# A one-core decoder step: the last down projection takes tokens 256 to 519 first, and the final norm is scaled on three engines and stored partly as half rows

## The chip, the cores and the metric

The kernel runs on one core of one Trainium2 chip. The metric is the time of the program on the device in microseconds (us), shown as the median of several runs. A profiled execution has a time of its own and a span, which runs from its first to its last instruction; all rows below are from that execution, in microseconds from the start of its span.

## The reference, cut to what matters

One decoder layer is computed for 512 prompt tokens and 8 sample tokens (520 in all) of width 1024: a norm, an input projection, block-sparse attention and mLSTM side by side, an output projection, and a squared-ReLU MLP. A last RMS norm over each token's 1024 values gives the two main outputs:

```python
hn = rmsnorm(x, ln2_w)
x = x + jnp.square(jax.nn.relu(hn @ w_up)) @ w_down
...
y_prompt = rmsnorm(xp, lnf_w)      # (1, 512, 1024)
y_sample = rmsnorm(xs, lnf_w)      # (8, 1, 1024)
```

where `rmsnorm` multiplies a token's row by the reciprocal square root of its mean square (plus 1e-6) and by the weights. The change touches nothing but the end of the MLP's down projection and this last norm.

## The kernel before, in words

Each engine has a program of its own, in the order in which it is written; semaphores join them. TensorE (PE) multiplies, VectorE (DVE) and ScalarE (ACT) move results out of PSUM and do the elementwise work, GpSimd (POOL) splits weights and raises to powers, SyncE (SP) issues nearly all loads and the final stores.

The activations lie transposed in `xT`: 128 partitions, 8 feature tiles, 520 tokens. The last phase of the MLP (`down_last`) runs over the 8 feature tiles `t`. Each tile has two token halves of 260, `H0` and `H1`, and each half is 24 matmuls: 8 steps `k`, each as three products of high and low parts (`down_part`). When a half is done, DVE adds it to `xT` (`evac_add`), ACT squares it into `y_sq` (`y_square`), and DVE adds the squares of tiles 0 to 6 up in `y_sum` (`add_squares`).

The final norm works by token tiles, numbered 0 to 3 (128 prompt tokens each) and 4, called `NT` (the 8 samples):

- `y_to_tok(i, part)`: PE transposes four feature tiles of token tile `i` into one PSUM bank. Part 0 (features 0 to 511) is done inside `down_last`, and DVE writes it, times the norm weights `lnf_b`, to the left half of `y_out` (`y_first`). Part 1 (features 512 to 1023) needs the last feature tile.
- `y_sums(part)`: PE multiplies `y_sum` and `y_sq` by a column of ones, which gives each token's sum of squares. Part 0 holds tiles 0 and 1 and stands inside the last half, after step 5; part 1 holds tiles 2, 3 and `NT` and waits for the square of the last half.
- `y_mean(part)`: DVE scales the sums to mean squares in `y_ms`; POOL raises them to the power -0.5 (`rsqrt`, counted by `s_y_pow`).
- DVE then multiplies the right half of a row by `y_ms` and `lnf_b` while it moves it out of PSUM, ACT multiplies the left half by `y_ms` (`y_scale`, counted by `s_y_half`), and SP stores whole rows of 4 KB, one DMA for each token tile, in the order 0, 1, 2, 3, `NT`.

PSUM banks of the final norm are handed out in the order of a list of jobs (`plan`); a job in the same bank waits until the job four places earlier has been read (`free`, `evacuated`).

Of the kernel before, what the change touches and what calls it, by code (L numbers as in the profile page):

```python
# [31 lines left out]
P = 128  # L32
# [43 lines left out]
Y_TILES = (0, 1), (2, 3, NT)  # L76
# [72 lines left out]
def plan():  # L149
# [107 lines left out]
    for part in range(2):  # L257
        job("ysum", part)
        for i in Y_TILES[part]:
            job("yt", i, 1)  # L260
# [132 lines left out]
def build(nc, x_prompt, x_sample, cache_k, cache_v, page_table, state_C, state_n, state_m, ln1_w, w_in,  # L393
# [4 lines left out]
    with ctx:  # L398
# [276 lines left out]
        s_y_half = sem("y_half")  # L675
        s_y_stored = sem("y_stored")
# [118 lines left out]
        def _(sp):  # L795
# [115 lines left out]
        def _(pe):  # L911
# [429 lines left out]
            def y_sums(part):  # L1341

                pe.wait_ge(s_y_added, KT - 2)
                pe.wait_ge(s_y_sq, KT + part)
                out = open_job(pe, "ysum", part)
                for i in Y_TILES[part]:
                    n = P if i < NT else NS
                    cols = slice(i * P, i * P + n)
                    pe.matmul(out[0:n, i:i + 1], y_sum[:, cols], ones[:, :], start=True, stop=False)
                    mm = pe.matmul(out[0:n, i:i + 1], y_sq[:, 1, cols], ones[:, :], start=False, stop=True)  # L1350
                done(mm)
# [60 lines left out]
            def down_part(b, half, n, k, first, last, signal):  # L1412

                out, cols = mlp_bank(b)[:, 0:MH_TOK], (H0, H1)[half]
# [7 lines left out]
            def down(d, i=0):  # L1422

                pe.wait_ge(s_hs_lo, 4 * (d + 1) + 8 * i)
                for t in range(8):
                    n = FIRST["down", d] + t
                    lo_made(pe, n, i)
                    for half in range(2):
                        bank_free("down", d, 2 * t + half, i)
                        for k in range(4):  # L1430
                            down_part(BANKS["down", d, 2 * t + half][0], half, n, 4 * (d % 2) + k, k == 0, k == 3,
                                      None if k < 3 else s_u_done if half else s_dn0)

            def down_last():

                for t in range(8):
# [8 lines left out]
                    for half, k in steps:  # L1445
# [4 lines left out]
                        down_part(2 * (t % 2) + half, half, n + k // 4, k, k == 0, k == KT - 1,  # L1450
                                  s_u_done if half and k in (3, 7) else s_dn0 if k == KT - 1 else None)
                        if t == 7 and half == 1 and k == 5:
                            y_sums(0)
# [53 lines left out]
        def _(act):  # L1507
# [349 lines left out]
            def down(kind, d, i=0):  # L1857

                for t in range(8):
# [6 lines left out]
                    elif kind == "last":  # L1866
                        for half in range(2):
                            y_square(t, (H0, H1)[half], 16 * 6 + 2 * t + half + 1)
# [9 lines left out]
            def y_scale(i):  # L1878

                n = P if i < NT else NS  # L1880
                evacuated(act, "yt", i, 0)
                act.wait_ge(s_y_pow, 1 if i in Y_TILES[0] else 3 if i == NT else 2)
                act.activation(y_out[0:n, i, 0:512], y_out[0:n, i, 0:512], ACT.Copy, scale=y_ms[0:n, i:i + 1])\
                   .then_inc(s_y_half, 1)
# [20 lines left out]
            for i in range(NT + 1):  # L1905
                y_scale(i)
# [12 lines left out]
        def _(pool):  # L1919
# [143 lines left out]
            for what, e in PHASES[11:]:  # L2063
                phase(what, e)
            evacuated(pool, "ysum", 0)
            rsqrt(y_ms[:, 0:2], P, 2).then_inc(s_y_pow, 1)
# [6 lines left out]
        def _(dve):  # L2073
# [445 lines left out]
            def evac_add(kind, d, t, half):  # L2519

                x = xT[:, t, (H0, H1)[half]]
                dve.tensor_tensor(x, mlp_bank(BANKS[kind, d, 2 * t + half][0])[:, 0:MH_TOK], x, ALU.add)\  # L2522
# [219 lines left out]
            def y_mean(part):  # L2742
                out = full(dve, "ysum", part)
                if part == 0:
                    free(dve.tensor_scalar(y_ms[:, 0:2], out[:, 0:2], 1.0 / D, EPS, ALU.mult, ALU.add), "ysum", 0)
                else:
                    dve.tensor_scalar(y_ms[:, 2:NT], out[:, 2:NT], 1.0 / D, EPS, ALU.mult, ALU.add)\
                       .then_inc(s_y_ms_ok, 1)
                    dve.tensor_scalar(y_ms[0:NS, NT:NT + 1], out[0:NS, NT:NT + 1], 1.0 / D, EPS, ALU.mult, ALU.add)\
                       .then_inc(s_y_ms_ok, 1)  # L2750
# [15 lines left out]
            for part in range(2):  # L2766
                if part == 1:
                    y_mean(1)
                for i in Y_TILES[part]:
                    n = P if i < NT else NS  # L2770
                    out = full(dve, "yt", i, 1)
                    dve.wait_ge(s_y_pow, 1 if part == 0 else 3 if i == NT else 2)
                    free(dve.scalar_tensor_tensor(out=y_out[0:n, i, 512:D], in0=out[0:n, :],
                                                  scalar=y_ms[0:n, i:i + 1], in1=lnf_b[0:n, 512:D],
                                                  op0=ALU.mult, op1=ALU.mult), "yt", i, 1)
# [26 lines left out]
```

## Time and profile before

| | before |
|---|---|
| time, median of 3 runs | 699.6 us (699.0 to 699.85) |
| time of the profiled execution | 699.11 us |
| its span | 697.4 us |
| PE, DVE, ACT, POOL busy | 681.3, 449.9, 296.3, 322.6 us |
| granted TensorE clock | 1.000 |

The profiled execution takes 1.7 us longer than its span. The busy times are sums over the whole span; the change lies in its last 15 us, so the rows that matter are those of that stretch.

### The profile page before, as it was taken

The page shows a single profiled execution, that of the slowest core. Times are in us where ns is not written, and L with a number is a line of the kernel's source. Part 1 is how long each engine was busy: PE and PEld are TensorE (multiplying, and loading weights), DVE is VectorE, ACT ScalarE, POOL GpSimd, SP SyncE. Part 2 cuts the span into 40 slices and gives each one's busy share as a digit, 9 for nine tenths or more (in the row PEclk, how much of TensorE's full clock was granted, in tenths as well). Part 3 has the DMA queues.
Part 4 walks back from the last instruction along what each step waited for, and adds up shares of the span by engine and source line. Part 5 has one row for each costly group of instructions (what it writes and reads, how often), then busy time and mean ns, then how long its engine had stood idle before and what let it go on. Part 6 is the DMA issues. An engine that isn't in the chain of part 4 may idle for free.

```text
span 697.4 us, 15167 instructions
## 1 busy us (share of the span) xinstructions
PE 681.3 (98%) x5547; PEld 638.8 (92%) x5547; DVE 449.9 (65%) x894; ACT 296.3 (42%) x568; POOL 322.6 (46%) x232
## 2 busy tenths in 40 slices
PE   6999999999999999999999999999999999999996
PEld 6999988788687777999999999999999999999996
DVE  4598899986243456537798685867557576585134
ACT  6532735465342233245555443343433534334222
POOL 6739999823231544247337517062260623507431
PEclk9999999999999999999999999999999999999999
DMA  7946999944486788623111323332241331413103
GB/s 246 303 122 168 281 282 277 277 136 116 143 254 204 239 283 172 168 81 122 61 59 64 121 70 127 109 118 86 87 124 69 120 108 66 130 61 121 61 1 124
DMA packets 88633, 100.41 MB, mean 144 GB/s; under 512 B 5374, under 2 KB 64338, under 8 KB 88570
## 3 DMA queue, kind: packets, MB, share of 16 engines
q1 hardware_dynamic: 74566, 92.91, 42.9%
q10 hardware_dynamic: 14004, 6.67, 4.1%
q8 instruction: 39, 0.64, 0.4%
q14 instruction: 24, 0.20, 0.1%
HBM read 92.92 MB, written 6.64 MB: 143 GB/s over the span
## 4 chain that ended last, share of the span: by engine, by line
PE 80%; DVE 10%; issue 3%; POOL 3%; ACT 2%; DMA 1%; DVEq 0%; POOLq 0%; ACTq 0%
PE acc L914 7%; PE acc L915 6%; PE acc L916 6%; PE acc L1417 5%; PE acc L1418 5%; PE acc L1416 5%; PE scr L1417 3%; PE scr L1418 3%; PE scr L1416 3%; PE scr L1383 3%; PE scr L1382 3%; PE scr L1384 3%; PE acc L1382 3%; PE acc L1383 3%; PE acc L1384 3%
## 5 line engine op out<-in xcount | busy, mean ns | idle before, releaser
L914 PE MATMUL acc<-act_hi,w_hi 128*128 128x256 f32 (+1 forms) x416 | 120.8, 290 | 1.1 <-DVE zT L2503 1.1
L2017 POOL TENSOR_TENSOR h_lo<-relu,h_hi 128x520 fp32r<-128x520 f32 x32 | 44.0, 1379 | 164.8 <-ACT h_hi L1803 164.5
L915 PE MATMUL acc<-act_lo,w_hi 128*128 128x256 f32 (+1 forms) x416 | 117.3, 282 | 0.0
L916 PE MATMUL acc<-act_hi,w_lo 128*128 128x256 f32 (+1 forms) x416 | 117.2, 282 | 0.0
L1502 POOL TENSOR_TENSOR w_lo<-raw,w_hi 128x1024 fp32r<-128x1024 f32 x24 | 57.2, 2387 | 97.6 <-ACT w_hi L1495 95.2
L1970 POOL TENSOR_TENSOR prod<-kv,Qb 128x1024 f32<-128x1024 f32 x32 | 85.7, 2714 | 14.1 <-DVE S L2205 11.1
L914 PEld LDWEIGHTS acc<-act_hi,w_hi 128*128 128x128 f32 x416 | 78.4, 188 | 4.0 <-issue 2.3
L915 PEld LDWEIGHTS acc<-act_lo,w_hi 128*128 128x128 f32 x416 | 78.4, 189 | 0.5
L916 PEld LDWEIGHTS acc<-act_hi,w_lo 128*128 128x128 f32 x416 | 78.3, 188 | 0.0
L2522 DVE TENSOR_TENSOR xT<-acc,xT 128x260 f32<-128x260 f32 x64 | 26.7, 426 | 48.4 <-PE acc L1418 48.4
L2503 DVE TENSOR_TENSOR zT<-acc,rstd 128x264 f32<-128x264 f32 (+1 forms) x56 | 23.5, 421 | 43.1 <-PE acc L916 40.4
L1416 PE MATMUL acc<-h_hi,w_hi 128*128 128x260 f32 x176 | 49.9, 283 | 0.0
L1495 ACT ACTIVATE w_hi<-raw 128x1024 fp32r<-128x1024 f32 x36 | 37.8, 1056 | 28.2 <-PE acc L916 14.0
L1417 PE MATMUL acc<-h_lo,w_hi 128*128 128x260 f32 x176 | 49.7, 282 | 0.0
L1418 PE MATMUL acc<-h_hi,w_lo 128*128 128x260 f32 x176 | 49.7, 282 | 0.0
L1791 ACT ACTIVATE w_hi<-w_sum 128x512 fp32r<-128x512 f32 x35 | 21.4, 628 | 65.0 <-DVE w_sum L2537 50.2
L2024 POOL TENSOR_TENSOR w_lo<-raw,w_hi 128x512 fp32r<-128x512 f32 x21 | 31.0, 1491 | 37.8 <-ACT w_hi L1791 37.8
L1802 ACT ACTIVATE relu<-relu 128x520 f32<-128x520 f32 x32 | 20.3, 636 | 64.8 <-DVE relu L2610 64.7
L2205 DVE TENSOR_REDUCE S<-prod 128x16 f32<-128x1024 f32 x32 | 38.4, 1210 | 8.2 <-POOL prod L1970 8.1
L1417 PE MATMUL acc<-h_lo,u_hi 128*128 128x260 f32 x144 | 40.7, 283 | 0.0
L1417 PE MATMUL scr<-h_lo,w_hi 128*128 128x260 f32 x144 | 40.7, 283 | 0.0
L1416 PE MATMUL acc<-h_hi,u_hi 128*128 128x260 f32 x144 | 40.7, 282 | 0.0
(418 smaller groups left out, 2298.4 us busy)
## 6 DMA issues: line engine op xcount, KB each, us to landing
kv<-in_cache_k_dram SPq DMA_DIRECT2D x64, 256.0 KB, 3.4
kv<-in_cache_v_dram SPq DMA_DIRECT2D x64, 256.0 KB, 3.1
raw<-in_w_up_dram SPq DMA_DIRECT2D x16, 1024.0 KB, 5.5
raw_d<-in_w_down_dram SPq DMA_DIRECT2D x12, 1024.0 KB, 5.1
raw<-in_w_in_dram SPq DMA_DIRECT2D x14, 512.0 KB, 6.0
raw<-in_w_in_dram SPq DMA_DIRECT2D x7, 1024.0 KB, 7.4
x_tok<-in_x_prompt_dram SPq DMA_DIRECT2D x8, 512.0 KB, 5.3
raw<-in_w_out_dram SPq DMA_DIRECT2D x4, 1024.0 KB, 7.3
```

Source lines behind the costliest of these rows:

```text
L914: pe.matmul(out, W_HI[home(g)][:, k, :], hi[k][:, cols], start=(n == 0), stop=False)
L915: pe.matmul(out, W_HI[home(g)][:, k, :], lo[k][:, cols], start=False, stop=False)
L916: mm = pe.matmul(out, W_LO[home(g)][:, k, :], hi[k][:, cols], start=False, stop=(n == KT - 1))
L1382: pe.matmul(out, u_hi[n % RING][:, k, :], hi[k], start=(k == 0), stop=False)
L1383: pe.matmul(out, u_hi[n % RING][:, k, :], lo[k], start=False, stop=False)
L1384: mm = pe.matmul(out, u_lo[n % RING][:, k, :], hi[k], start=False, stop=(k == 3))
L1416: pe.matmul(out, w[0], h_hi[:, k, cols], start=first, stop=False)
L1417: pe.matmul(out, w[0], h_lo[:, k, cols], start=False, stop=False)
L1418: mm = pe.matmul(out, w[1], h_hi[:, k, cols], start=False, stop=last)
L1502: eng.tensor_tensor(W_LO[home(g)], raw[:, r_slot, :, side * P:(side + 1) * P], W_HI[home(g)].bitcast(F32), ALU.subtract).then_inc(s_w_lo_o ...
L1970: pool.tensor_tensor(prod[:, n % 2, :].rearrange("p (j n) -> p j n", j=2), kv[:, 2 * c:2 * c + 2, :], Qb[:, b % 2:b % 2 + 1, :].to_broadca ...
L2017: pool.tensor_tensor(h_lo[:, t, :], relu2[:, t % 2, :], h_hi[:, t, :].bitcast(F32), ALU.subtract).then_inc(s_hs_lo, 1)
```

## The change

In the last phase, the two halves of a tile become tokens 256 to 519 (264 of them, first) and tokens 0 to 255 (256, last). The first sums of squares are those of tiles 2, 3 and `NT`, after step 3 of the last half. The sums of tiles 0 and 1 are made in two jobs, `ypre` (tiles 0 to 6, which doesn't wait for the last square) and `ysum` 1 (the last feature tile alone), and DVE joins them. The left half of tile 2 and all of the samples' last factors go to POOL; ACT takes the left halves of tiles 3, 0 and 1 and moves the samples' right half out of PSUM. Tiles 2 and 3 are stored as whole rows by SP, tiles 0 and 1 as two half rows each: the left one by ACT's queue, the right one by SP's. SP's order is 2, 3, 0, `NT`, 1.

```diff
-Y_TILES = (0, 1), (2, 3, NT)
+Y_SPLIT = slice(2 * P, TOK), slice(0, 2 * P)
+Y_TILES = (2, 3, NT), (0, 1)
...
-            for i in range(NT + 1):
-                sp.wait_ge(s_y_half, i + 1)
+            for i in (2, 3, 0, NT, 1):
+                if i == NT:
+                    sp.wait_ge(s_y_pool, 3)
+                    sp.dma_start(y_sample[:, 0, :], y_out[0:NS, i, :]).then_inc(s_y_stored, 16)
+                    continue
                 evacuated(sp, "yt", i, 1)
-                if i < NT:
+                if i >= 2:
+                    if i == 2:
+                        sp.wait_ge(s_y_pool, 1)
+                    else:
+                        sp.wait_ge(s_y_half, 1)
                     sp.dma_start(y_prompt[0, i * P:(i + 1) * P, :], y_out[:, i, :]).then_inc(s_y_stored, 16)
                 else:
-                    sp.dma_start(y_sample[:, 0, :], y_out[0:NS, i, :]).then_inc(s_y_stored, 16)
-            sp.wait_ge(s_y_stored, 16 * (NT + 1))
+                    sp.dma_start(y_prompt[0, i * P:(i + 1) * P, 512:D], y_out[:, i, 512:D]).then_inc(s_y_stored, 16)
+            sp.wait_ge(s_y_stored, 16 * (NT + 3))
...
                 pe.wait_ge(s_y_added, KT - 2)
+                if part == 1:
+                    out = open_job(pe, "ypre")
+                    for i in Y_TILES[1]:
+                        mm = pe.matmul(out[:, i:i + 1], y_sum[:, i * P:(i + 1) * P], ones[:, :], start=True, stop=True)
+                    done(mm)
+                    for i in (2, 3):
+                        y_to_tok(i, 1)
                 pe.wait_ge(s_y_sq, KT + part)
...
-                        if t == 7 and half == 1 and k == 5:
+                        if t == 7 and half == 1 and k == 3:
                             y_sums(0)
...
             pe.wait_ge(s_dn_evac, N_DOWN - 1)
-            for i in Y_TILES[0]:
-                y_to_tok(i, 1)
             y_sums(1)
+            y_to_tok(NT, 1)
             pe.wait_ge(s_dn_evac, N_DOWN)
             for i in Y_TILES[1]:
                 y_to_tok(i, 1)
...
+            def y_scale(i, pows, nth):
+
                 evacuated(act, "yt", i, 0)
-                act.wait_ge(s_y_pow, 1 if i in Y_TILES[0] else 3 if i == NT else 2)
...
+                act.wait_ge(s_y_pow, pows)
+                x = y_out[:, i, 0:512]
+                act.activation(x, x, ACT.Copy, scale=y_ms[:, i:i + 1]).then_inc(s_y_half, 1)
+                if i < 2:
+                    act.wait_ge(s_y_half, nth)
+                    act.dma_start(y_prompt[0, i * P:(i + 1) * P, 0:512], x).then_inc(s_y_stored, 16)
...
-            for i in range(NT + 1):
-                y_scale(i)
+            y_scale(3, 1, 1)
+            act.wait_ge(s_y_pow, 2)
+            y_samples()
+            y_scale(0, 3, 2)
+            y_scale(1, 3, 3)
...
+            pool.wait_ge(s_y_ms_ok, 1)
+            rsqrt(y_ms[:, 2:NT], P, 2).then_inc(s_y_pow, 1)
             evacuated(pool, "ysum", 0)
+            rsqrt(y_ms[0:NS, NT:NT + 1], NS, 1).then_inc(s_y_pow, 1)
...
+                x = y_out[0:n, i, 0:512]
+                pool.tensor_tensor(x, x, y_ms[0:n, i:i + 1].to_broadcast([n, 512]), ALU.mult).then_inc(s_y_pool, 1)
+
+            y_scale(2, P, 1)
+            pool.wait_ge(s_y_ms_ok, 2)
             rsqrt(y_ms[:, 0:2], P, 2).then_inc(s_y_pow, 1)
-            pool.wait_ge(s_y_ms_ok, 2)
-            rsqrt(y_ms[:, 2:NT], P, 2).then_inc(s_y_pow, 1)
-            rsqrt(y_ms[0:NS, NT:NT + 1], NS, 1).then_inc(s_y_pow, 1)
+            y_scale(NT, NS, 2)
+            pool.wait_ge(s_y_nt, 1)
+            x = y_out[0:NS, NT, 512:D]
+            pool.tensor_tensor(x, x, lnf_b[0:NS, 512:D], ALU.mult).then_inc(s_y_pool, 1)
...
+                    dve.scalar_tensor_tensor(out=y_ms[:, 0:2], in0=out[:, 0:2], scalar=1.0 / D, in1=y_ms[:, 0:2],
+                                             op0=ALU.mult, op1=ALU.add).then_inc(s_y_ms_ok, 1)
```

PE from the last matmul ahead of the first sums of squares to its end, before (`ones` with `y_sum` or `y_sq` are the sums of squares, `ident` with `xT` the transposes; line numbers are each kernel's own):

```order
L1418 MATMUL acc<-h_hi,w_lo 128x260
L1349 MATMUL scr<-ones,y_sum 128x1 [waits scr_free0,y_sq,y_added]
L1350 MATMUL scr<-ones,y_sq 128x1
...
L1338 MATMUL scr<-ident,xT 128x128 [waits scr_free1,dn_evac]
L1338 MATMUL scr<-ident,xT 128x128 [waits scr_free2]
L1349 MATMUL scr<-ones,y_sum 128x1 [waits scr_free3,y_sq,y_added]
L1349 MATMUL scr<-ones,y_sum 8x1
L1338 MATMUL scr<-ident,xT 128x128 [waits scr_free0,dn_evac]
L1338 MATMUL scr<-ident,xT 8x128 [waits scr_free2]
```

The same stretch of PE in the changed kernel:

```order
L1439 MATMUL acc<-h_hi,w_lo 128x256
L1370 MATMUL scr<-ones,y_sum 128x1 [waits scr_free0,y_sq,y_added]
L1371 MATMUL scr<-ones,y_sq 128x1
L1370 MATMUL scr<-ones,y_sum 8x1
...
L1360 MATMUL scr<-ones,y_sum 128x1 [waits scr_free1,y_added,dn_evac]
L1351 MATMUL scr<-ident,xT 128x128 [waits scr_free2]
L1351 MATMUL scr<-ident,xT 128x128 [waits scr_free3]
L1371 MATMUL scr<-ones,y_sq 128x1 [waits scr_free0,y_sq]
L1351 MATMUL scr<-ident,xT 8x128 [waits scr_free1]
L1351 MATMUL scr<-ident,xT 128x128 [waits scr_free2,dn_evac]
```

Six matmuls of the last half moved behind the first sums, which now hold the samples too; the `ypre` job went in between the last half and the first transposes.

POOL's last rows, before and in the changed kernel:

```order
L2024 TENSOR_TENSOR w_lo<-raw,w_hi 128x512 [waits u_hi] x7
L2024 TENSOR_TENSOR u_lo_109<-raw,u_hi_106 128x512 [waits u_hi]
L2024 TENSOR_TENSOR w_lo<-raw,w_hi 128x512 [waits u_hi] x2
L1922 TENSOR_TENSOR y_ms<-y_ms,power 128x2 [waits scr_free0]
L1922 TENSOR_TENSOR y_ms<-y_ms,power 128x2 [waits y_ms_ok]
L1922 TENSOR_TENSOR y_ms<-y_ms,power 8x1
```

```order
L1953 TENSOR_TENSOR y_ms<-y_ms,power 128x2 [waits y_ms_ok]
L1953 TENSOR_TENSOR y_ms<-y_ms,power 8x1 [waits scr_free0]
L2106 TENSOR_TENSOR y_out<-y_out,y_ms 128x512 [waits y_pow,scr_free1]
L1953 TENSOR_TENSOR y_ms<-y_ms,power 128x2 [waits y_ms_ok]
L2106 TENSOR_TENSOR y_out<-y_out,y_ms 8x512 [waits y_pow,scr_free3]
L2114 TENSOR_TENSOR y_out<-y_out,lnf_b 8x512 [waits y_nt]
```

Three multiplications of 512 columns joined the three powers; the samples' two stand last.

SP's final stores, before and in the changed kernel:

```order
L904 DMA out_dram<-y_out 128x1024 [waits scr_free1,y_half]
L904 DMA out_dram<-y_out 128x1024 [waits scr_free2,y_half]
L904 DMA out_dram<-y_out 128x1024 [waits scr_free0,y_half]
L904 DMA out_dram<-y_out 128x1024 [waits scr_free1,y_half]
L906 DMA out_dram<-y_out 8x1024 [waits scr_free2,y_half]
```

```order
L917 DMA out_dram<-y_out 128x1024 [waits y_pool,scr_free2]
L917 DMA out_dram<-y_out 128x1024 [waits y_half,scr_free3]
L919 DMA out_dram<-y_out 128x512 [waits scr_free2]
L909 DMA out_dram<-y_out 8x1024 [waits y_pool]
L919 DMA out_dram<-y_out 128x512 [waits scr_free3]
```

The samples' store moved ahead of the last prompt tile's, and the last two prompt stores are half as wide; their other halves are two new stores of 128x512 in ACT's program.

## Rows read from the trace of the kernel before

**Rows 1.** The page's head: span, and busy us of each engine.

```profile
span 697.4 us, 15167 instructions
...
PE 681.3 (98%) x5547; PEld 638.8 (92%) x5547; DVE 449.9 (65%) x894; ACT 296.3 (42%) x568; POOL 322.6 (46%) x232
```

**Rows 2.** The chain of waits, last 12 us: start, us, what.

```profile
692.67 0.65 DVE y_out L2773
```

**Rows 3.** Timeline of DVE, ACT, POOL, SP: start, us, engine, line, operation; waits in brackets.

```profile
687.95 0.43 DVE L2522 TENSOR_TENSOR xT<-acc,xT 128x260 f32<-128x260 f32 x1 [0.67 <-PE acc L1418]
688.39 1.41 DVE L2773 SCALAR_TENSOR_TENSOR y_out<-scr,y_ms,lnf_b 128x512 f32<-128x512 f32 x2
...
691.26 2.06 DVE L2773 SCALAR_TENSOR_TENSOR y_out<-scr,y_ms,lnf_b 128x512 f32<-128x512 f32 x3 [0.88 <-POOL y_ms L1922]
...
685.26 0.42 ACT L1775 ACTIVATE y_sq<-xT 128x260 f32<-128x260 f32 x1 [3.30 <-DVE xT L2522]
688.41 0.42 ACT L1775 ACTIVATE y_sq<-xT 128x260 f32<-128x260 f32 x1 [2.73 <-DVE xT L2522]
688.74 1.32 ACT L1883 ACTIVATE y_out<-y_out,y_ms 128x512 f32<-128x512 f32 x2
...
687.36 0.70 POOL L1922 TENSOR_TENSOR y_ms<-y_ms,power 128x2 f32<-128x2 f32 x1 [15.01 <-DVE y_ms L2745]
690.46 1.20 POOL L1922 TENSOR_TENSOR y_ms<-y_ms,power 128x2 f32<-128x2 f32 x2 [2.40 <-DVE y_ms L2749]
...
689.47 3.61 SPq L904 DMA_DIRECT2D out_dram<-y_out  x4
693.39 0.43 SPq L906 DMA_DIRECT2D out_dram<-y_out  x1
```

**Rows 4.** Windows of the end: busy time by engine, PEclk, DMA share, GB/s.

```profile
690.30:691.60 1.30, 1.29 (x12) 0.93 (x10) 0.42 (x3) 0.35 (x1) 1.14 (x2) 1.00 0.99 400
694.20:695.50 1.30, 0.00 (x0) 0.00 (x0) 0.00 (x0) 0.00 (x0) 0.00 (x0) 1.00 1.02 403
696.00:696.60 0.60, 0.00 (x0) 0.00 (x0) 0.00 (x0) 0.00 (x0) 0.00 (x0) 1.00 0.05 14
696.60:697.40 0.80, 0.00 (x0) 0.00 (x0) 0.00 (x0) 0.00 (x0) 0.00 (x0) 0.70 0.00 0
```

**Rows 5.** Timeline of PE, its weight loads (PEld) and one DVE row.

```profile
683.99 0.28 PE L1416 MATMUL acc<-h_hi,w_hi 128*128 128x260 f32 x1
...
686.02 0.31 PEld L1349 LDWEIGHTS scr<-ones,y_sum 128*128 128x128 f32 x2
...
686.91 0.19 PEld L1416 LDWEIGHTS acc<-h_hi,w_hi 128*128 128x128 f32 x1
...
687.64 0.90 PEld L1338 LDWEIGHTS scr<-ident,xT 128*128 128x128 f32 x8
...
688.90 0.30 PEld L1349 LDWEIGHTS scr<-ones,y_sum 128*128 128x128 f32 x2 [0.35 <-issue]
...
690.06 1.24 PEld L1338 LDWEIGHTS scr<-ident,xT 128*128 128x128 f32 x12
...
690.17 0.16 DVE L2747 TENSOR_SCALAR y_ms<-scr 128x2 f32<-128x2 f32 x1 [0.37 <-PE scr L1350]
```

**Rows 6.** Groups of PE instructions by shape: count, busy us, mean ns.

```profile
L915 PE MATMUL acc<-act_lo,w_hi 128*128 128x256 f32 x224 | 62.8, 281 | 0.0
...
L915 PE MATMUL acc<-act_lo,w_hi 128*128 128x264 f32 x192 | 54.5, 284 | 0.0
```

**Rows 7.** Groups of POOL instructions by shape, of the whole span.

```profile
L1970 POOL TENSOR_TENSOR prod<-kv,Qb 128x1024 f32<-128x1024 f32 x32 | 85.7, 2714 | 14.1 <-DVE S L2205 11.1 <-ACT Qb L1562 1.9 <-DMA kv<-in_cache_k_dram 1.0
...
L2024 POOL TENSOR_TENSOR w_lo<-raw_d,w_hi 128x512 fp32r<-128x512 f32 x30 | 38.5, 1308 | 0.0
...
L1995 POOL TENSOR_TENSOR Cs_z<-Cs_z,sm_b 128x512 f32<-128x512 f32 x4 | 4.1, 1048 | 0.0
```

**Rows 8.** A window of loads in rows of 2 KB, columns as in rows 4.

```profile
504.00:506.00 2.00, 2.00 (x19) 2.00 (x19) 0.86 (x2) 0.74 (x2) 2.00 (x3) 1.00 1.04 404
```

More of the change, by code:

```diff
@@ L256, in plan @@
         job("yt", i, 0)
[L257 to L260, printed above, removed]
+    job("ysum", 0)
+    job("ypre")
+    for i in (2, 3):
+        job("yt", i, 1)
+    job("ysum", 1)
+    for i in (NT, 0, 1):
+        job("yt", i, 1)
     return tasks, jobs
@@ L1348, in y_sums @@
                     cols = slice(i * P, i * P + n)
-                    pe.matmul(out[0:n, i:i + 1], y_sum[:, cols], ones[:, :], start=True, stop=False)
-                    mm = pe.matmul(out[0:n, i:i + 1], y_sq[:, 1, cols], ones[:, :], start=False, stop=True)
+                    if part == 0:
+                        pe.matmul(out[0:n, i:i + 1], y_sum[:, cols], ones[:, :], start=True, stop=False)
+                    mm = pe.matmul(out[0:n, i:i + 1], y_sq[:, 1, cols], ones[:, :], start=(part == 1), stop=True)
                 done(mm)
@@ L1410, in plain, with down_part @@
                         norm_to_rows()
-            def down_part(b, half, n, k, first, last, signal):
-                out, cols = mlp_bank(b)[:, 0:MH_TOK], (H0, H1)[half]
+            def down_part(b, cols, n, k, first, last, signal):
+                out = mlp_bank(b)[:, 0:cols.stop - cols.start]
                 w = u_hi[n % RING][:, k % 4, :], u_lo[n % RING][:, k % 4, :]
@@ L2519, in evac_add @@
             def evac_add(kind, d, t, half):
-                x = xT[:, t, (H0, H1)[half]]
-                dve.tensor_tensor(x, mlp_bank(BANKS[kind, d, 2 * t + half][0])[:, 0:MH_TOK], x, ALU.add)\
+                cols = (Y_SPLIT if kind == "last" else (H0, H1))[half]
+                x = xT[:, t, cols]
+                dve.tensor_tensor(x, mlp_bank(BANKS[kind, d, 2 * t + half][0])[:, 0:cols.stop - cols.start], x, ALU.add)\
                    .then_inc(s_dn_evac, 1)
@@ L2743, in y_mean @@
                 out = full(dve, "ysum", part)
[L2744 to L2750, printed above, removed]
+                if part == 1:
+                    evacuated(dve, "ypre")
+                    dve.scalar_tensor_tensor(out=y_ms[:, 0:2], in0=out[:, 0:2], scalar=1.0 / D, in1=y_ms[:, 0:2],
+                                             op0=ALU.mult, op1=ALU.add).then_inc(s_y_ms_ok, 1)
+                    return
+                dve.tensor_scalar(y_ms[:, 2:NT], out[:, 2:NT], 1.0 / D, EPS, ALU.mult, ALU.add).then_inc(s_y_ms_ok, 1)
+                free(dve.tensor_scalar(y_ms[0:NS, NT:NT + 1], out[0:NS, NT:NT + 1], 1.0 / D, EPS, ALU.mult, ALU.add),
+                     "ysum", 0)
             def y_first(i):
@@ L2765, in _ @@
                 phase(what, e)
-            for part in range(2):
-                if part == 1:
+            out = full(dve, "ypre")
+            free(dve.tensor_scalar(y_ms[:, 0:2], out[:, 0:2], 1.0 / D, EPS, ALU.mult, ALU.add), "ypre")
+            for i in (2, 3, 0, 1):
+                if i == 3:
                     y_mean(1)
[L2769 to L2775, printed above, removed]
+                out = full(dve, "yt", i, 1)
+                dve.wait_ge(s_y_pow, 1 if i >= 2 else 3)
+                free(dve.scalar_tensor_tensor(out=y_out[:, i, 512:D], in0=out[:, :], scalar=y_ms[:, i:i + 1],
+                                              in1=lnf_b[:, 512:D], op0=ALU.mult, op1=ALU.mult), "yt", i, 1)
 _INS = ["x_prompt", "x_sample", "cache_k", "cache_v", "page_table", "state_C", "state_n", "state_m", "ln1_w",
```

19 lines of the change are left out of this document (12 added, 7 removed).

## The prediction

> **What bounds the kernel now.** I read the page's head first [rows 1], then the chain of waits [rows 2], the timeline of each engine over the last 15 us [rows 3], the windows of that stretch [rows 4], and PE's timeline [rows 5]. PE is busy for 681.3 of the 697.4 us [rows 1], and the change leaves its work alone up to the last half of the last feature tile; only the tail counts. The chain of waits names DVE's last multiplication, which ends at 693.32 [rows 2]. That is misleading: the span ends 4.1 us later, at 697.4, and the windows say why. From 690.3 to 695.5, in each stretch of 1.3 us of which the first and the last are shown, the 16 DMA engines are busy for 0.99 to 1.02 of the time and move 400 GB/s [rows 4]. One token tile is 0.524 MB, so 1.31 us, and four tiles are 5.2 us, which is that whole stretch. SP issues its first store at 689.47 [rows 3], packets run 0.83 us later, and from there on the tail is a queue of stores: compute that finishes earlier inside it gains nothing. Behind the four tiles come the eight sample rows, 32 KB alone on the engines, and they are slow: the last packets run until 696.6 [rows 4], 1.1 us after the bulk. From there to the end of the span are 0.8 us without a packet [rows 4]. So three numbers make the end: when the first store is issued, 2.13 MB at 400 GB/s, and what follows the last bulk packet.
>
> **The change part by part, in the clock of this trace.**
>
> *Widths.* A matmul of 256 columns is 281 ns, one of 264 is 284 [rows 6]; halves of 260 and 260 become 264 and 256, so a tile costs the same. The first half of the last tile ends about 0.04 late, the second catches up.
>
> *First sums after step 3.* The last half starts at 683.99, and 18 matmuls later, at 686.02, PE loads for the first sums [rows 5]: 0.113 us each. After 12 it is there at 683.99 + 0.04 + 1.36 = 685.39. It needs the square of the first half, which ACT ends at 685.26 + 0.42 = 685.68 [rows 3], 0.04 later now; from ACT's other half square (end 688.83) to PE's load (688.90) were 0.07 [rows 3, 5]. So PE waits until 685.79, a new stall of 0.4 us, with the last 12 matmuls queued behind it. Before, that wait was covered by the six matmuls that are now behind. The sums of three tiles took from 688.90 to 690.06, 1.16 us [rows 5], against 0.89 for two (686.02 to 686.91). The matmuls go on at 686.95, as before at 686.91, but there are 12 instead of 6: 0.7 us more. The last half ends 0.7 us late, and PE is free at 687.64 + 0.74 = 688.38; DVE adds the half at 688.68 instead of 687.95.
>
> *`ypre` and the transposes.* Two tiles with one product each are half of 0.89, so 0.45: PE's transposes of tile 2 start at 688.83. Before, from the first transpose load (687.64) to DVE's multiplication out of that bank (688.39) were 0.75 [rows 3, 5], so DVE starts on tile 2 at 689.58 and ends at 690.33, by 0.75 for one (2.06 for three with overlap [rows 3]). SP follows 0.07 later, as after the last tile (693.32 to 693.39 [rows 3]): first store at **690.40**, 0.93 us later than 689.47.
>
> *POOL's share of the first store.* The first sums reach DVE 1.27 after their load (688.90 to 690.17 [rows 5]), at 687.06, and POOL's power can start at 687.3, as before (687.36). Two powers take 1.20 [rows 3], to 688.5. Then the multiplication of tile 2 by a broadcast column: the nearest row is the state decay, 128x512 by a broadcast, 1.05 us; two full operands take 1.31 [rows 7]. It ends between 689.5 and 689.8. It costs nothing, since DVE's multiplication (690.33) covers it; the first store would feel it only if it ran over 0.5 us longer, and then by the excess. ACT's tile 3 (0.71, half of 1.32 with overlap) ends near 690.2, under the same cover.
>
> *Second sums.* The last half's square ends at 688.68 + 0.45 + 0.42 = 689.55; PE is in its transposes until 689.71 (8 in 0.90 [rows 5]), then sums two tiles in 0.45. DVE's joined `y_ms` follows at about 690.4 (0.16), POOL's power at 690.6, done at 691.3 against 691.16 before: 0.15 late. DVE's tiles 0 and 1 end at 692.15 and 692.85, ACT's left halves at 692.25 and, behind its own store issue (0.4, as SP's last one, 0.43 [rows 3]), at 693.4.
>
> *Samples.* POOL multiplies them twice after 691.3. Partition count is no measure of time on DVE (its three rows of 2.06 include the 8-row one [rows 3]); for POOL I take the full-width rows, 1.05 and 1.31 [rows 7]: done at 693.7. SP's sample store is issued at 693.7, takes 0.43 [rows 3], and the right half of tile 1 waits behind it on SP's queue until 694.15.
>
> *Do the stores arrive in time?* Engines: tile 2 from 690.40 + 0.83 = 691.23, then tile 3 until 693.85, tile 0 until 695.16, tile 1's left half until 695.8. Packets of tile 3 are there at 692.1, of tile 0 at 693.1, of tile 1's left half at 694.3, of its right half at 694.98. Each is earlier than its turn, so the stretch has no gap. Rows of 2 KB ran at 404 GB/s at a DMA share of 1.04 [rows 8], so half rows cost nothing; the second queue's issue on ACT saves SP 0.35 us that nobody waits for.
>
> *Sum.* 691.23 + 2.13 MB / 400 GB/s (5.3) = 696.55; the sample rows now lie in the middle. They took 1.1 us at the end; on the way they cost between 0 (the other queue fills in) and 1.1 us (the last half row waits behind them on their engines). I take 0.3, nearer to the lower end, as ACT's half row lies in another queue. Plus 0.8 to the end: 697.65 against 697.4, so **+0.25 us**: the first store costs 0.93, the sample tail gives 1.1 back, and 0.3 and roundings return. On the profiled 699.11 that is 699.4; the median shown is 0.5 above the profiled run, so I say 699.9.
>
> **A rule against the change.** The windows show all 16 engines busy with one queue alone [rows 4], so a second queue has nothing to fill. The Trainium skill, "DMA: Bandwidth & Descriptors", section "Issuing engines are not separate DMA queues", says the same in general: transfers started by several engines run on the same 16 DMA engines, and only the starter's time is saved. By that rule the sum stands; without it the first rival below would be the forecast. No run here shows two queues in this stretch.
>
> **The rivals.**
>
> *A second queue adds bandwidth.* ACT's two half rows, 0.52 MB, move beside SP's stores: 5.3 becomes 4.0, the end 696.35, and the time 698.6 (-1.05). For it: two queues have never been seen in this tail. Against it: a share of 0.99 to 1.02 [rows 4]. Chance 0.08.
>
> *The sample rows stand in the way in full.* The last half row is issued behind them on the same queue; 0.8 us more, 700.7. For it: SP's order, and their 1.1 us for 32 KB [rows 4]. Chance 0.15.
>
> *SP is held by POOL (slower).* SP can't issue tile 1's right half before POOL's two sample multiplications. The engines want it by 691.23 + 4.68 = 695.9, so issued by 695.1 and the pair done by 694.6: it decides once the pair takes over 3.3 us. If each took what 128x1024 takes, 2.71 [rows 7], the pair would end at 696.7, the half row be issued at 697.2, and with 0.83, 0.65 for its packets and 0.8 the end is 699.5: +2.1, 701.7. For it: these are POOL's first 8-row multiplications of this length, and rows there spread. Against it: 1.05 to 1.31 for full width. Chance 0.10.
>
> **How the numbers follow.** My forecast, a queue of stores that starts 0.9 later and ends about where it did, has 0.67. Its own range: the first store up to 0.45 earlier if PE's wait is not there, and 0.3 later if DVE is slowed beside POOL; the sample rows 0 instead of 0.3, or up to 0.8 more; so 699.1 to 701.0, with 0.3 on either side for how runs spread (699.0 to 699.85 before). For 8 times in 10 I give 698.8 to 701.0. 0.2%, 1.4 us, is about what a measurement of this kernel can tell from no change. Faster than 698.2: a little of the first rival, 0.05. Slower than 701.0: most of the third and a little of the second, 0.10. Same: 0.85.
>
> **What would show it.** In the profile after: PE idle for about 0.4 us ahead of the first sums; the last half's evacuation 0.7 late; first store near 690.4; DMA share near 1 from 691.2 without a hole until about 696.5; POOL's sample pair near 2.4 us; the last packets no longer a thin tail of 1.1 us. I would be wrong if the stretch had holes, if the first store came near 689.5, or if the tail after the bulk stayed as long.

## The result, and the profile after

| | before | after |
|---|---|---|
| time, median | 699.0 us (22 runs) | 700.33 us (22 runs, 699.56 to 701.5) |
| profiled execution, its span | 699.11, 697.4 us | 700.07, 698.3 us |
| first store issued | 689.47 | 690.31 |
| first and last packet of the stores | 690.33, 696.65 | 691.17, 697.49 |
| last packet to end of span | 0.74 | 0.86 |

The ratio is 1.0018, with a 95% interval of 1.0012 to 1.0024: within the 0.2% that the prediction called no change, but over 22 runs a small slowdown that is clear of 1. The two profiled executions differ by 0.96 us, the medians by 1.3. (A packet is what one DMA engine moves in one record, here one row of 4 KB or one half row of 2 KB. Here and below, first and last packet are start and end of the first and last record among the DMA packets behind 688.5 us.) Two runs of the kernels below were far slower at a lower granted clock (a3 1113.18 us at 0.56, a4 742.57 us at 0.85), and their medians and ratios leave them out.

The timeline of the changed kernel, last 14 us: start, us, engine, line, operation, waits in brackets.

```profile
685.82 0.30 PEld L1370 LDWEIGHTS scr<-ones,y_sum 128*128 128x128 f32 x2 [0.39 <-issue]
...
688.38 0.53 PEld L1360 LDWEIGHTS scr<-ones,y_sum 128*128 128x128 f32 x4
688.75 0.94 PEld L1351 LDWEIGHTS scr<-ident,xT 128*128 128x128 f32 x8
...
684.25 0.70 DVE L2786 TENSOR_TENSOR y_sum<-y_sum,y_sq 128x520 f32<-128x520 f32 x1 [1.63 <-PE acc L1439]
...
688.70 0.42 DVE L2568 TENSOR_TENSOR xT<-acc,xT 128x256 f32<-128x256 f32 x1 [1.40 <-PE acc L1439]
...
689.53 0.75 DVE L2820 SCALAR_TENSOR_TENSOR y_out<-scr,y_ms,lnf_b 128x512 f32<-128x512 f32 x1 [0.34 <-PE scr L1351]
...
687.32 1.22 POOL L1953 TENSOR_TENSOR y_ms<-y_ms,power 128x2 f32<-128x2 f32 x2 [14.95 <-DVE y_ms L2795]
688.52 1.03 POOL L2106 TENSOR_TENSOR y_out<-y_out,y_ms 128x512 f32<-128x512 f32 x1
...
691.22 1.03 POOL L2106 TENSOR_TENSOR y_out<-y_out,y_ms 8x512 f32<-8x512 f32 x1
692.21 1.26 POOL L2114 TENSOR_TENSOR y_out<-y_out,lnf_b 8x512 f32<-8x512 f32 x1
...
690.31 1.22 SPq L917 DMA_DIRECT2D out_dram<-y_out  x2
...
693.50 0.31 SPq L909 DMA_DIRECT2D out_dram<-y_out  x1
693.85 0.74 SPq L919 DMA_DIRECT2D out_dram<-y_out  x1
```

Read against [rows 3, 5], the front is what was predicted: PE waits 0.39 us ahead of the first sums, the last half is added at 688.70 (predicted 688.68), DVE reaches tile 2 at 689.53 (689.58), the first store goes at 690.31 (690.40). POOL's left half of tile 2 ends at 689.55, under DVE's cover. Its two sample multiplications take 1.03 and 1.26 us, as long as full-width rows; they end at 693.47, SP issues the samples at 693.50 (693.7), and the right half of tile 1 follows at 693.85 (694.15).

The windows of the end of the changed kernel, columns as in [rows 4].

```profile
691.20:692.50 1.30, 0.66 (x4) 0.42 (x4) 1.14 (x2) 0.92 (x2) 1.30 (x3) 1.00 1.00 403
692.50:693.80 1.30, 0.00 (x0) 0.00 (x0) 0.27 (x1) 0.72 (x1) 0.97 (x1) 1.00 1.00 392
693.80:695.10 1.30, 0.00 (x0) 0.00 (x0) 0.00 (x0) 0.00 (x0) 0.00 (x0) 0.84 1.01 377
695.10:696.40 1.30, 0.00 (x0) 0.00 (x0) 0.00 (x0) 0.00 (x0) 0.00 (x0) 0.50 1.01 314
696.40:696.60 0.20, 0.00 (x0) 0.00 (x0) 0.00 (x0) 0.00 (x0) 0.00 (x0) 0.50 1.00 369
696.60:697.00 0.40, 0.00 (x0) 0.00 (x0) 0.00 (x0) 0.00 (x0) 0.00 (x0) 0.50 0.51 195
697.00:697.50 0.50, 0.00 (x0) 0.00 (x0) 0.00 (x0) 0.00 (x0) 0.00 (x0) 0.50 0.17 61
697.50:698.30 0.80, 0.00 (x0) 0.00 (x0) 0.00 (x0) 0.00 (x0) 0.00 (x0) 0.50 0.00 0
```

There is no hole, as predicted. But the stretch is no shorter. From 695.1 the engines are busy at 314 GB/s instead of about 400: some packets take long. Then, where the kernel before has a thin tail [rows 4], there is a thick one that fades: 0.51, then 0.17. From first to last packet are 6.32 us in both kernels. The store queue starts 0.84 us later, takes as long, and that is the loss but for 0.12 us behind the last packet. (Over all profiles here that last gap is 0.73 to 1.16 us, so the 0.12 may be scatter.) The prediction had the stretch 0.8 us shorter (1.1 given back, 0.3 kept). The experiments ask where these 0.8 us stayed.

### The profile page after: what moved, and what is told of

It reads as the page before. It is cut to its first block, busy times and chain, and to the rows that moved or that the text cites. A ratio compares the mean times of both kernels' runs of the same rounds, so it can differ in the third digit from the quotient of the medians.

```text
span 698.3 us, 15169 instructions
## 1 busy us (share of the span) xinstructions
PE 681.8 (98%) x5547; PEld 639.4 (92%) x5547; DVE 449.3 (64%) x894; ACT 295.9 (42%) x567; POOL 326.0 (47%) x235
## 4 chain that ended last, share of the span: by engine, by line
PE 78%; DVE 10%; POOL 4%; issue 3%; ACT 2%; DMA 1%; SPq 0%; POOLq 0%; ACTq 0%; DVEq 0%
PE acc L927 6%; PE acc L928 6%; PE acc L929 6%; PE acc L1438 5%; PE acc L1437 5%; PE acc L1439 5%; POOL prod L2001 4%; PE scr L1438 3%; PE scr L1439 3%; PE scr L1437 3%; PE scr L1404 3%; PE scr L1403 3%; PE scr L1405 3%; PE acc L1403 3%; PE acc L1405 3%
## 5 line engine op out<-in xcount | busy, mean ns | idle before, releaser
L2568 DVE TENSOR_TENSOR xT<-acc,xT 128x260 f32<-128x260 f32 (+1 forms) x64 | 26.7, 427 | 49.2 <-PE acc L1439 49.2
L1437 PE MATMUL acc<-h_hi,w_hi 128*128 128x260 f32 (+2 forms) x176 | 50.0, 284 | 0.0
L1438 PE MATMUL acc<-h_lo,w_hi 128*128 128x260 f32 (+2 forms) x176 | 49.7, 283 | 0.0
L1439 PE MATMUL acc<-h_hi,w_lo 128*128 128x260 f32 (+2 forms) x176 | 49.7, 282 | 0.0
L1437 PE MATMUL acc<-h_hi,u_hi 128*128 128x260 f32 (+2 forms) x144 | 40.7, 283 | 0.0
L1438 PE MATMUL acc<-h_lo,u_hi 128*128 128x260 f32 (+2 forms) x144 | 40.7, 283 | 0.0
```

What stands on the lines that cost most here:

```text
L1437: pe.matmul(out, w[0], h_hi[:, k, cols], start=first, stop=False)
L1438: pe.matmul(out, w[0], h_lo[:, k, cols], start=False, stop=False)
L1439: mm = pe.matmul(out, w[1], h_hi[:, k, cols], start=False, stop=last)
```

## The experiments

The profiled executions differ in how early they come to the tail at all (by up to 1.6 us, from work ahead of the change). So I count from the start of DVE's last adding of squares (684.19 in the kernel before, 684.25 after), called A here:

```profile
684.19 0.70 DVE L2740 TENSOR_TENSOR y_sum<-y_sum,y_sq 128x520 f32<-128x520 f32 x1 [1.60 <-PE acc L1418]
```

"Store" is the first store's issue behind A, "stretch" first to last packet, "slowest" the longest 4-KB packet in it. A ratio is to runs of the kernel before on the same chip and comes from all of them, so it is not quite the quotient of two medians; medians of before were 699.11 us for the first four kernels, 698.87 for the next four, 699.09 for three, 699.03 for the last.

| kernel | median us | ratio (95%) | store | stretch | slowest ns |
|---|---|---|---|---|---|
| before | 699.0 | 1 | 5.28 | 6.32 | 953 |
| after | 700.33 | 1.0018 (1.0012, 1.0024) | 6.06 | 6.32 | 898 |
| a1_no_sample_store | 699.94 | 1.0013 (1.0004, 1.0021) | 6.07 | 5.94 | 200 |
| a2_sample_rows_spread | 700.04 | 1.0013 (1.0004, 1.0022) | 6.07 | 6.12 | 647 |
| a3_sums_after_step_5 | 699.77 | 1.0010 (1.0002, 1.0019) | 5.63 | 6.31 | 933 |
| a4_whole_rows | 700.34 | 1.0018 (1.0010, 1.0027) | 6.07 | 6.21 | 1041 |
| b1_before_no_sample | 698.75 | 0.9997 (0.9988, 1.0006) | 5.28 | 5.80 | 262 |
| b2_whole_rows_no_sample | 699.57 | 1.0010 (1.0001, 1.0019) | 6.06 | 5.81 | 351 |
| b5_half_rows_one_queue | 700.12 | 1.0015 (1.0006, 1.0024) | 6.06 | 5.91 | 335 |
| b3_step_5_transposes_first | 699.88 | 1.0013 (1.0004, 1.0022) | 5.64 | 6.32 | 701 |
| c1_order_alone | 699.48 | 1.0009 (1.0000, 1.0018) | 5.51 | 6.10 | 989 |
| c2_tile_2_on_act | 699.91 | 1.0007 (0.9998, 1.0016) | 5.22 | 6.69 | 816 |
| c3_before_rows_spread | 698.82 | 0.9996 (0.9987, 1.0005) | 5.28 | 5.98 | 355 |
| d1_order_two_sums | 699.06 | 1.0000 (0.9991, 1.0009) | 5.26 | 6.08 | 898 |

An interval is some 0.6 us to either side, so the ratios tell only the larger steps apart; the columns of the profile carry the argument, with one profile for each kernel. I take them to be good to about 0.1 us: three kernels with whole rows and the sample store in the middle gave 6.08, 6.10 and 6.21.

**The theory and the rival at first.** Mine: the sample store in the middle stands in the way, and the changed kernel without it ends like the kernel before. The rival: half rows or the second queue make the stretch longer.

**a1_no_sample_store**: the sample output is left out.

```
-sp.dma_start(y_sample[:, 0, :], y_out[0:NS, i, :]).then_inc(s_y_stored, 16)
```

> The changed kernel without the store of the eight sample rows (y_sample is not written). My theory: the tail is a queue of stores on busy DMA engines, and the samples' slow packets hold up what is queued behind them in full. Then the first store stays near 690.3, the last packet comes near 696.6 instead of 697.5, the span is 697.4 instead of 698.3, and the ratio to the kernel before is about 1.0005. Rival, half rows in two queues are what is slow: last packet near 697.4, span 698.2, ratio 1.0017.

Missed: the stretch fell by 0.38 us, not by 0.8 or more, and its windows still end in a tail. The sample rows are a part of the cause only.

**a2_sample_rows_spread**: the sample output gets eight rows of tile 3, from partitions 16 apart.

```
-sp.dma_start(y_sample[:, 0, :], y_out[0:NS, i, :])
+sp.dma_start(y_sample[:, 0, :], y_out[0:P:16, 3, :])
```

> The changed kernel, but the sample store takes eight rows that lie 16 partitions apart (rows of token tile 3, so y_sample's values are not the reference's) in place of eight rows on partitions 0 to 7. Same bytes, same place in the queue, same wait. If the slowness comes from eight rows that lie on neighbouring partitions, their packets take about 0.16 us each like the others, the span is about 697.5 and the ratio 1.0006. If any store of eight rows is slow, packets stay at up to 0.9 us, span 698.3, ratio 1.0018.

Between the two: the stretch is 0.2 shorter and the slowest packet 647 ns instead of 898. Where the rows lie matters, and c3 asks the same at the end of the queue.

**a3_sums_after_step_5**: only the place of the first sums is turned back.

```
-if t == 7 and half == 1 and k == 3:
+if t == 7 and half == 1 and k == 5:
```

> The changed kernel with the first sums of squares back after step 5 of the last half. My theory: PE's new wait of 0.4 us is gone, the last half ends 0.4 earlier, the first store comes at 689.9 instead of 690.3, and as the stores run without a hole the span falls by the same 0.4 to 697.9; ratio 1.0012. Rival, the end hangs on the samples' work on POOL or on the second sums: then they move by less, since the first sums come 0.2 later, and the span stays within 0.1 of 698.3.

Confirmed. Its timeline:

```profile
685.95 0.31 PEld L1370 LDWEIGHTS scr<-ones,y_sum 128*128 128x128 f32 x2
...
688.96 0.75 DVE L2820 SCALAR_TENSOR_TENSOR y_out<-scr,y_ms,lnf_b 128x512 f32<-128x512 f32 x1 [0.34 <-PE scr L1351]
...
689.75 1.21 SPq L917 DMA_DIRECT2D out_dram<-y_out  x2
```

The weight load of the first sums has no wait beside it any more, and the first store comes 0.43 us sooner behind A, which is that wait to within 0.04. The stretch is the same.

**a4_whole_rows**: tiles 0 and 1 stored as whole rows by SP, no store on ACT.

```
-sp.dma_start(y_prompt[0, i * P:(i + 1) * P, 512:D], y_out[:, i, 512:D])
+sp.wait_ge(s_y_half, i + 2)
+sp.dma_start(y_prompt[0, i * P:(i + 1) * P, :], y_out[:, i, :])
...
-act.dma_start(y_prompt[0, i * P:(i + 1) * P, 0:512], x)
```

> The changed kernel with tiles 0 and 1 stored as whole rows by SP alone, as before the change; nothing else moves. My theory: engines are busy either way, so the span moves by no more than 0.2 (698.1 to 698.4), ratio 1.0015 to 1.0018. Rival, the half rows in two queues cost the tail its rate (383 GB/s instead of 400 and a thin end): span 697.5, ratio 1.0007.

As expected, 0.1 us. With a1 this left two readings: each alone hides the other, or both are small and something else holds the end. The next three were made for that.

**b1_before_no_sample** is the kernel before, and **b2_whole_rows_no_sample** a4, both without the sample store (the sample output is left out).

> The kernel before without its store of the sample rows. Theory A (the sample store, last in the queue, costs the kernel before about a microsecond, since its few packets run alone after the rest): first store to last packet falls from 7.17 us to about 6.2, the time by 0.8 to 1.0 us, ratio about 0.9987. Rival B (what stands between the first store and the end hardly depends on the sample rows, as the changed kernel without its sample store has suggested, with 0.4 us): first store to last packet 6.8 or more, the time at most 0.4 us less, ratio 0.9994 or more.

> The changed kernel with tiles 0 and 1 stored as whole rows by SP and without the sample store, so two edits that have been run apart (first store to last packet 7.17 us with neither, 7.07 with whole rows alone, 6.79 without the sample store alone). Theory A (either of them is enough to fill the end of the stretch, so that each alone gives little and both together give what they cost): 6.1 to 6.3 us, ratio about 1.0003 to the kernel before. Rival B (the two are independent and small): 6.7 us, ratio 1.0012.

Both stretches are 5.80 and 5.81 us. So with equal traffic the two kernels store equally fast, and all that is left between them is the front: 6.06 against 5.28, 0.78 us, and medians 0.82 us apart (ratios of 1.0010 and 0.9997). The expectations count from the first store's issue: there b1 has 6.66 us, between theory A (6.2) and rival B (6.8 or more), and 0.1 us in the median, not 0.8; b2 has 6.67, its rival B. This is the point at which the prediction had erred. The windows at the end of b1:

```profile
694.03:695.33 1.30, 0.00 (x0) 0.00 (x0) 0.00 (x0) 0.00 (x0) 0.00 (x0) 0.75 1.02 406
695.33:695.60 0.27, 0.00 (x0) 0.00 (x0) 0.00 (x0) 0.00 (x0) 0.00 (x0) 0.50 0.06 15
695.60:696.00 0.40, 0.00 (x0) 0.00 (x0) 0.00 (x0) 0.00 (x0) 0.00 (x0) 0.50 0.05 20
```

There is no sample row in this kernel, and yet the same thin tail at a share of 0.05, as in [rows 4]: three 4-KB packets of the last tile, one behind the other, run 0.45 us longer than the rest (0.49 in b2). I had put the whole of that tail down to the samples. Their price at the end of the queue is 6.32 - 5.80 = 0.52 us.

A share of 0.06 is one engine of 16. Why one engine is late without any sample row was not tested. Each of these traces also has one 8-KB packet of a queue called `instruction` among the stores; the DMA view of b1 from 690.1 to 696 us counts it:

```profile
q14 instruction: 1, 0.01, 0.6%
```

It took 0.54 us in b1 and 0.31 in b2, and the engine that moved it had its rows of the stores to move as well. That this engine is the late one is likely, not shown.

**b5_half_rows_one_queue**: a1 with ACT's two half stores moved to SP (no sample output).

> The changed kernel without the sample store, and with the left halves of tiles 0 and 1 stored by SP instead of ACT: 2-KB rows still, but one queue. If it is the second queue that slows the stretch: first store to last packet about 6.2 us, as with whole rows. If it is the 2-KB rows, or the store of 1.2 us more by SP's own issues: 6.8 us, as with two queues. My estimate is the former, ratio about 1.0005.

Missed: 5.91, as with two queues (5.94); from the first store's issue 6.77, where 6.2 was expected. The second queue neither helps nor harms. Half rows cost 0.10 to 0.13 us (5.91 and 5.94 against 5.81), little more than what single profiles differ by. The Trainium skill, "DMA: Bandwidth & Descriptors", section "Issuing engines are not separate DMA queues", says that starting transfers from a second engine adds no DMA engine; 5.91 against 5.94 agrees.

**b3_step_5_transposes_first**: a3, with the transposes of tiles 2 and 3 ahead of `ypre`, and DVE's tile 2 ahead of its operation on it.

```
     pe.wait_ge(s_y_added, KT - 2)
     if part == 1:
+        for i in (2, 3):
+            y_to_tok(i, 1)
         out = open_job(pe, "ypre")
...
-        for i in (2, 3):
-            y_to_tok(i, 1)
```

> The changed kernel with the first sums of squares behind step 5, as run before (its first store stood at 689.75 us and its time 0.5 us below the changed kernel's), and with TensorE's transposes of tiles 2 and 3 ahead of the four sums for tiles 0 and 1, VectorE's scaling of tile 2 ahead of its operation on these sums. Theory A (the end stands at a fixed distance behind the first store): VectorE's scaling of tile 2 starts right behind the last evacuation, 0.4 us earlier, the first store at 689.35, the span 0.4 us shorter than with step 5 alone, ratio about 1.0004. Rival C (the second half's chain of squares, sums and scalings, which waits 0.4 us longer now, sets the end): the first store moves and the last packet does not, ratio 1.0010.

Neither came: the first store did not move (5.64). The timeline says why.

```profile
688.61 0.75 DVE L2820 SCALAR_TENSOR_TENSOR y_out<-scr,y_ms,lnf_b 128x512 f32<-128x512 f32 x1
...
687.50 1.21 POOL L1953 TENSOR_TENSOR y_ms<-y_ms,power 128x2 f32<-128x2 f32 x2 [15.22 <-DVE y_ms L2795]
...
688.69 1.03 POOL L2106 TENSOR_TENSOR y_out<-y_out,y_ms 128x512 f32<-128x512 f32 x1
...
689.80 1.25 SPq L917 DMA_DIRECT2D out_dram<-y_out  x2
```

DVE is done at 689.36, 5.20 us behind A instead of 5.59 in a3. But now POOL's two powers and its half of tile 2 end last, at 689.72, and the store goes 0.08 later. In a3 that half ended 5.56 us behind A, hidden by DVE by only 0.03:

```profile
688.65 1.03 POOL L2106 TENSOR_TENSOR y_out<-y_out,y_ms 128x512 f32<-128x512 f32 x1
```

**c2_tile_2_on_act**: b3 with the left half of tile 2 on ACT ahead of its last squares, and whole rows.

```
     for half in range(2):
+        if half == 1:
+            y_scale(2, 1, 1)
         y_square(t, Y_SPLIT[half], 16 * 6 + 2 * t + half + 1)
```

> The changed kernel with sums behind step 5 and transposes first, as run, and now the left half of tile 2 scaled by ScalarE ahead of its last squares instead of by GpSimd, and whole rows by SP for tiles 0 and 1. Theory A (in the run with transposes first GpSimd's 1.21 us of powers and 1.03 us of scaling took over as what the first store waits for): the first store comes 5.25 us behind the start of the last adding of squares, against 5.64 in that run and 5.28 in the kernel before; first to last packet 6.2 us; ratio 0.9999 to 1.0002. Rival (VectorE or something else holds tile 2): first store at 5.6 us, ratio 1.0008.

POOL was the reason: the first store comes at 5.22. But the stretch is 6.69 us, which I had not expected. Two of its windows:

```profile
692.00:692.20 0.20, 0.20 (x4) 0.20 (x3) 0.00 (x0) 0.20 (x1) 0.20 (x1) 1.00 0.14 41
...
693.60:693.80 0.20, 0.00 (x0) 0.00 (x0) 0.01 (x1) 0.00 (x0) 0.11 (x1) 1.00 0.07 21
```

The queue has run dry twice. The second sums wait for the delayed squares, and DVE's tile 3 behind them starts 5.95 us behind A instead of 5.76 (b3), while the first store goes 0.42 sooner; so tiles 3 and 0 are not ready when the engines want them. What the front gained the holes took.

**c1_order_alone**: the kernel before, with nothing but the order turned (tiles 2, 3, sample, 0, 1 everywhere).

```
-Y_TILES = (0, 1), (2, 3, NT)
+Y_SPLIT = slice(2 * P, TOK), slice(0, 2 * P)
+Y_TILES = (2, 3, NT), (0, 1)
...
-for i in range(NT + 1):
-    sp.wait_ge(s_y_half, i + 1)
+for nth, i in enumerate((2, 3, NT, 0, 1)):
+    sp.wait_ge(s_y_half, nth + 1)
```

> The kernel before with nothing but the order turned: the last phase's columns split as 264 and 256, tiles 2, 3, sample, 0, 1 in this order on every engine and in the store queue. The first sums stay behind step 5, sums in one job each, all stores whole rows by SP, scalings on VectorE and ScalarE. Theory A (the changed kernel loses at its front, by where its sums stand and by what is ahead of tile 2; the packets of the sample store cost about the same 0.4 to 0.5 us in the middle of the stretch as at its end, since each holds up its own DMA engine, whose share of the later rows is fixed): the last adding of squares to first store 5.3 us as before, first to last packet 6.2 us against 6.32, time 0.1 us below before, ratio 0.9998, not to be told from 1. Rival B (turning the order costs by itself): first store 0.4 us or more later, ratio 1.0008 or more. Rival C (a sample store in the middle is free if the rows are whole and one queue carries them): first to last packet 5.8 us, ratio 0.9993.

The first store is 0.23 us later than before, between theory A and rival B; the stretch is 0.22 shorter, nearer to theory A than to rival C. Here is the cause of the former, in its weight loads:

```profile
685.78 0.31 PEld L1350 LDWEIGHTS scr<-ones,y_sum 128*128 128x128 f32 x2
...
686.77 0.10 PEld L1350 LDWEIGHTS scr<-ones,y_sum 128*8 128x8 f32 x2
686.81 0.11 PEld L1351 LDWEIGHTS scr<-ones,y_sq 128*8 128x8 f32 x2
686.95 0.19 PEld L1417 LDWEIGHTS acc<-h_hi,w_hi 128*128 128x128 f32 x1
```

The first sums take 1.17 us where they took 0.89 [rows 5], since the sample tile is now in the job that stands in the last half's way. The median (699.48) is 0.4 above that of before, which this profile doesn't explain; the interval reaches down to 1.0000.

**d1_order_two_sums**: c1, with the sample's sums back in the second job, and tile 0 ahead of the sample.

```
-Y_TILES = (2, 3, NT), (0, 1)
+Y_TILES = (2, 3), (0, 1, NT)
...
-for nth, i in enumerate((2, 3, NT, 0, 1)):
+for nth, i in enumerate((2, 3, 0, NT, 1)):
```

> The kernel before with the order turned (tiles 2, 3, 0, sample, 1 on the engines and in the store queue), and with the sample tile's sums back in the second job, so that the job behind step 5 is as long as in the kernel before (two tiles, four pairs of products: 0.89 us there, 1.17 us with the sample tile in the run of the order alone). Theory A: the last adding of squares to first store 5.28 us as before (5.51 in the run of the order alone), first to last packet 6.1 us as in that run (6.32 before), time 0.2 us below before, ratio 0.9997. Rival: the order costs something else, first store at 5.5 us, ratio 1.0005 or more.

Store and stretch are as expected, 5.26 and 6.08, and its span ends 12.94 us behind A, where that of before ends 13.20 behind. The ratio is 1.0000: a quarter of a microsecond is less than eleven runs can show. It beats the changed kernel; that it beats the kernel before is not shown. Two windows of its end:

```profile
694.11:695.41 1.30, 0.00 (x0) 0.00 (x0) 0.00 (x0) 0.00 (x0) 0.00 (x0) 1.00 0.99 331
...
695.80:696.29 0.49, 0.00 (x0) 0.00 (x0) 0.00 (x0) 0.00 (x0) 0.00 (x0) 0.89 0.23 92
```

**c3_before_rows_spread**: the kernel before, with a2's edit (the sample output gets other rows).

> The kernel before, with the sample store taking eight rows of tile 3 that lie 16 partitions apart instead of the sample tile's rows in partitions 0 to 7 (so the sample output is left out; same bytes, same place in the queue). If the slow packets of the sample store (up to 0.95 us each beside 0.17 for the others) come from reading eight neighbouring partitions: the slowest packet 0.65 us or less, first to last packet 6.1 us against 6.32, and 5.80 without the store. If they come from the destination or from being last: no change.

As the first theory has it: the slowest packet falls from 953 to 355 ns, the stretch from 6.32 to 5.98. Eight rows out of neighbouring partitions are slow to read, not slow by standing last. (The edit also reads other columns of `y_out`, which no run separates.) In the kernel before, by the order of its records, seven of the eight rows take 0.26 to 0.95 us while they run together, and the eighth, alone at the end, 0.16. The Trainium skill, "SBUF — State Buffer", section "Door 1: The DMA port swizzle (why `[64,N]` ≈ `[32,N]`)", has four neighbouring partitions share one of 16 DMA ports, so the sample's eight rows come through two ports, and the spread ones through four; the packets agree in direction, and no view here names a port.

## Why the prediction was right, and where it erred

The time was right: 699.9 us predicted, 700.33 measured, within the range and within 0.2%. The closeness is partly luck. The forecast change was +0.25 to +0.3 us, and 0.5 more came from the median of three runs of the kernel before (699.6); over 22 runs that median is 699.0, and the measured change is +0.96 us in the profiles and +1.3 in the medians. Most steps were right, one term was not.

- *First sums after step 3*: right. The wait is 0.39 us (0.4), and a3 takes it away and gets 0.43 back. (The 0.113 us for a matmul was counted from a matmul's start to a weight load; the loads follow each other by 0.119. Nothing hangs on it, since the square of the first half decides.)
- *Third tile in the first sums*: right. 0.28 us in c1 (0.27), and d1 takes it away and gets 0.25 back.
- *`ypre` ahead of the transposes*: right as a delay of DVE (0.37 us, 688.38 to 688.75, where 0.45 was predicted), but most of it is covered: in c1 the first store waits for ACT's left half anyway (done at about 689.45, DVE's right half at about 689.15). Of the front's 0.78 us (6.06 - 5.28), 0.12 is left for it (a3 against c1: 5.63 - 5.51), beside 0.43 and 0.23. That 0.12 belongs to `ypre` and to POOL's half of tile 2 together: with `ypre` moved away alone, POOL holds the store at the same place (b3); with both away it goes 0.42 us sooner (c2). POOL's half costs nothing in the changed kernel, as predicted: it ends 0.73 us ahead of DVE there.
- *POOL on the samples, SP held, the store queue without a hole*: right. The pair took 2.29 us (2.36 predicted). The rival with SP held by POOL fell.
- *A second queue adds bandwidth*: fell. It changes nothing (a1 against b5).
- *Half rows cost nothing*: nearly so, about 0.1 us (5.81 in b2 against 5.91 in b5, 6.21 in a4 against 6.32 in the changed kernel).
- *The sample tail*: this is the step that failed. The term "the sample tail gives 1.1 back, and 0.3 and roundings return" took the thin tail of [rows 4] for the samples' work, and read its length from the edge of a window: the other engines are done at 695.68, so it is 0.97 us. b1 shows 0.52 us of it as theirs; the other 0.45 is there without them, in packets of the last tile. One of the prediction's own signs of being wrong came with it: the tail behind the bulk stayed nearly as long, 0.83 us (696.66 to 697.49). And in the middle the samples cost 0.40 (a4 against b2) or 0.38 (the changed kernel against a1), 0.27 and 0.29 in the two other kernels with whole rows (6.08 and 6.10 against 5.81). So the 0.3 for the middle was about right, and the 1.1 for the end was twice too much (0.52): the move gives back 0.1 to 0.25 us, not 0.8. The second rival, samples in the way in full, had the nearer size for the wrong reason: they cost 0.27 to 0.40 us there, against 0.52 at the end and not 1.1.

With the terms as measured, the sum is 0.78 of front (0.84 with the 0.06 by which A itself is later), 0 from the stretch (0.1 gained from the samples, 0.1 lost to half rows) and 0.12 behind the last packet: 0.96, the difference of the two spans.

Why a store in the middle is not hidden can be read off in the main. A DMA share counts engines: the 0.51 in the changed kernel's fading tail is eight of 16. Counted from the packet records, about eight packets are still in flight after the other engines are done, in each of the seven kernels that store the rows of partitions 0 to 7 in the middle (a share of 0.50 in c1 from 695.70 to 696.00 us); without them it is one (0.06 in b2 from 696.26 to 696.75). So as many engines fall behind as there are sample rows, by up to 0.7 to 0.8 us, and the other eight are idle meanwhile: nothing takes the later rows over. The rates agree. Without the sample store the rate holds until the bulk is done, at 406 GB/s with whole rows (b1) and 378 with half rows (a1); with it, the last full window has 331 in d1 and 314 in the changed kernel. The Trainium skill, "DMA: Bandwidth & Descriptors", section "Why a DMA increments its semaphore by 16 and not by 1", says that a transfer is split among a number of engines that divides its rows, so that eight rows go to eight of the 16; the count of eight agrees. That each late engine is one that carried a sample row stays an inference, since no record here names the engine of a packet.

## What to carry to other kernels

When the tail of a kernel is a full queue of stores, count two numbers only: when the first store is issued, and how long the queue takes. Work that is finished earlier inside the stretch gives nothing as long as the queue doesn't run dry (in c2 it did). Whatever is put ahead of the first store is paid there, unless another engine ends later anyway: a wait moved in front of matmuls and a job of sums that grew were paid in full (0.43 and 0.25 us), of the `ypre` job's 0.37 us and POOL's half of a tile together 0.12.

Before you credit a change with removing a tail, run the kernel without the piece that you hold responsible. A thin tail behind a bulk of stores may be the bulk's own last packets, and a small store that costs half a microsecond at the end may cost more than half of that in the middle.

## What was not expected of the hardware

- A 4-KB packet of the sample store takes up to 0.95 us, where most others take about 0.16; read from partitions 16 apart, up to 0.36 at the end of the queue (c3) and 0.65 in its middle (a2).
- Without any sample row, the bulk ends with three packets one behind the other, 0.45 us (b1) and 0.49 us (b2) in which the other engines are idle.
- With the eight sample rows in the middle, eight of the 16 engines end up to 0.7 to 0.8 us after the other eight (a4, c1, d1, the changed kernel).
- PE's granted clock falls to 0.50, its level of 1.2 GHz, in the changed kernel's windows from 695.1 on, after its last transposes (in those of the kernel before it is at 1.00 until 696.6 [rows 4]); nothing is left for PE to do, so it costs nothing.
